# Last quarter of the second MLP matrix by Strassen's scheme, and the weight-block sums of all quarters on GpSimd

## What is computed

```
h = rms_norm(x, norm2_w[l])
x = x + jnp.square(jax.nn.relu(h @ w_up[l])) @ w_down[l]     # w_up 1024 x 4096, w_down 4096 x 1024
```

## Time and profile before

| | |
|---|---|
| median of three runs | 1588.47 us |
| profiled execution, span | 1587.5 us |
| TensorE busy | 1575.3 us, 99% |
| VectorE busy | 1011.7 us, 64% |
| ScalarE busy | 724.0 us, 46% |
| GpSimd busy | 0.2 us |
| share of TensorE in the chain that ended last | 95% |
| granted TensorE clock, mean | 0.999 |

### The profile page before, as it was taken

One profiled execution on the slowest core, in us unless ns is written; L12 is line 12 of the kernel. 1 busy time (PEld: TensorE's weight loads), 2 busy tenths in 40 slices (PEclk: granted clock), 3 DMA queues, 4 the chain that ended last, 5 costly groups with the idle time before them and its releaser, 6 DMA issues.

```text
span 1587.5 us, 21133 instructions
## 1 busy us (share of the span) xinstructions
PE 1575.3 (99%) x7576; PEld 1293.4 (81%) x7576; DVE 1011.7 (64%) x1431; ACT 724.0 (46%) x1109; POOL 0.2 (0%) x4
## 2 busy tenths in 40 slices
PE   8999999999999999999999999999999999999999
PEld 7877778888888888888887777788888888888887
DVE  5577774554456868696356776655455587787952
ACT  5557552323337363645345566432233464636350
POOL 0000000000000000000000000000000000000000
PEclk9999999999999999999999999999999999999999
DMA  6321222333351322323022212133323514141401
GB/s 225 112 81 54 84 76 80 106 107 102 108 188 54 124 89 106 107 86 131 9 72 98 89 54 81 53 107 106 106 80 106 186 54 163 50 159 54 156 4 53
DMA packets 109319, 153.22 MB, mean 97 GB/s; under 512 B 5120, under 2 KB 81440, under 8 KB 109216
## 3 DMA queue, kind: packets, MB, share of 16 engines
q1 hardware_dynamic: 108496, 151.27, 28.7%
q10 hardware_dynamic: 720, 0.61, 0.1%
HBM read 149.77 MB, written 2.10 MB: 96 GB/s over the span
## 4 chain that ended last, share of the span: by engine, by line
PE 95%; DVE 2%; ACT 1%; DMA 1%; issue 0%; SPq 0%; DVEq 0%; ACTq 0%
PE acc L541 19%; PE acc L543 19%; PE acc L542 19%; PE acc L563 6%; PE acc L565 6%; PE acc L564 6%; PE acc L592 5%; PE acc L594 5%; PE acc L593 5%; PE bank L729 1%; PE bank L748 1%; PE bank L740 1%; DMA raw<-in_w_in_dram 1%; PE bank L609 1%; DVE wl_rows L1051 1%; PE bank L701 0%
## 5 line engine op out<-in xcount | busy, mean ns | idle before, releaser
L541 PE MATMUL acc<-uh,wh 128*128 128x512 f32 x1152 | 452.8, 393 | 4.1 <-DVEq L1145 4.0
L543 PE MATMUL acc<-uh,wl 128*128 128x512 f32 x1152 | 449.1, 390 | 0.0
L542 PE MATMUL acc<-ul,wh 128*128 128x512 f32 x1152 | 449.1, 390 | 0.0
L541 PEld LDWEIGHTS acc<-uh,wh 128*128 128x128 f32 x1152 | 216.6, 188 | 53.7 <-issue 5.4
L827 ACT ACTIVATE wh<-raw 128x1024 fp32r<-128x1024 f32 x142 | 150.5, 1060 | 230.8 <-PE acc L543 151.3
L543 PEld LDWEIGHTS acc<-uh,wl 128*128 128x128 f32 x1152 | 216.6, 188 | 45.7
L542 PEld LDWEIGHTS acc<-ul,wh 128*128 128x128 f32 x1152 | 216.8, 188 | 44.1
L1051 DVE TENSOR_TENSOR wl<-raw,wh 128x1024 fp32r<-128x1024 f32 x142 | 174.0, 1225 | 82.4 <-ACT wh L827 71.4
L827 ACT ACTIVATE wh_rows<-raw_down 128x1024 fp32r<-128x1024 f32 x100 | 106.2, 1062 | 134.4 <-PE acc L594 35.2
L1051 DVE TENSOR_TENSOR wl_rows<-raw_down,wh_rows 128x1024 fp32r<-128x1024 f32 x100 | 122.5, 1225 | 59.3 <-ACT wh_rows L827 51.6
L1081 DVE TENSOR_TENSOR gate_tanh<-acc,rsqrt_rows 128x512 f32<-128x512 f32 x48 | 33.2, 691 | 116.2 <-PE acc L543 116.0
(11 more groups left out here) (235 smaller groups left out, 2449.1 us busy)
## 6 DMA issues: line engine op xcount, KB each, us to landing
raw<-in_w_in_dram SPq DMA_DIRECT2D x39, 1024.0 KB, 5.2
raw<-in_w_up_dram SPq DMA_DIRECT2D x32, 1024.0 KB, 5.7
raw_down<-in_w_down_dram SPq DMA_DIRECT2D x32, 1024.0 KB, 8.6
raw_branch<-in_w_in_dram SPq DMA_DIRECT2D x12, 1024.0 KB, 5.0
raw_branch<-in_w_branch_dram SPq DMA_DIRECT2D x12, 1024.0 KB, 5.0
raw_branch<-in_w_o_dram SPq DMA_DIRECT2D x8, 1024.0 KB, 5.0
x_tokens<-in_x_dram SPq DMA_DIRECT2D x8, 256.0 KB, 8.1
raw_kv<-in_w_in_dram SPq DMA_DIRECT2D x4, 512.0 KB, 4.8
```

What stands on the lines that cost most here:

```text
L541: nc.tensor.matmul(a[:], wh[slot][:, k, :], right_h, start=at_k == 0, stop=False)
L542: nc.tensor.matmul(a[:], wh[slot][:, k, :], right_l, start=False, stop=False)
L543: last = nc.tensor.matmul(a[:], wl[slot][:, k, :], right_h, start=False, stop=at_k == n - 1)
```

## The change

The last quarter becomes Strassen's scheme too: 14 `dn` units (`dn42` to `dn55`) take the place of `db` and `da`, with their hidden sums and with tiles that go into x directly where the running sums have already been folded. The words `ta` to `td` leave VectorE, and GpSimd makes the same eight sums in each of the eight quarters. The lists of all three engines are new from `wa3` on, and so is the order in which x is sent out.

```diff
-       + ([f"dn{14 * q + i}" for i in range(PRODUCTS * PAIRS)] if q < QUARTERS - 1 else
-          [f"{half}{i}" for half in ("db", "da") for i in range(4)])]
+       + [f"dn{14 * q + i}" for i in range(PRODUCTS * PAIRS)]]
...
-dn30 dn31 dn32 dn33 dn34 dn35 dn36 dn37 dn38 dn39 dn40 dn41 up24 up25 up26 up27 up28 up29 up30 up31 db0 db1 db2 db3
-da0.01 UT4 UT5 UT6 UT7 da0.23 da1 da2 da3""".split()
+dn30 dn31 dn32 dn33 dn34 dn35 dn36 dn37 dn38 dn39 dn40 dn41 up24 up25 up26 up27 up28 up29 up30 up31 dn42 dn43 dn44
+dn45 dn46 dn47 dn48 dn49 dn50 dn51 dn52 dn53 UT4 UT5 UT6 UT7 dn54 dn55""".split()
...
 ACT_LATE, third and fourth quarter:
++dn24 +dn25 +dn26 +dn27 +up16 +up17 rl16 hh16 +up18 rl17 +up19 +up20 +up21 +up22 rl18 rl19 dh2 hh17 hh18 hh19 +up23
+rl20 rl21 hh20 +dn28 +dn29 sh8 +dn30 sh9 rl22 +dn31 rl23 +dn32 sh10 hh21 +dn33 sh11 +dn34 +dn35 +dn36 +dn37 +dn38
++dn39 hh22 +dn40 hh23 +dn41 +up24 +up25 +up26 rl24 +up27 rl25 +up28 hh24 +up29 rl26 hh25 +up30 hh26 rl27 +up31 dh3
+rl28 +dn42 hh27 hh28 sh12 rl29 +dn43 hh29 sh13 rl30 hh30 +dn44 sh14 rl31 +dn45 hh31 sh15 +dn46 +dn47 +dn48 +dn49 +dn50
++dn51 +dn52 +dn53 +dn54 +dn55 UT4 +gq0 +gq1 UT5 UT6 UT7 +gk0""".split()
...
 DVE_LATE, third and fourth quarter:
++dn27 rs25 +up16 rs26 +up17 +up18 +up19 rs27 +up20 +up21 hl16 df2 +up22 dl2 hl17 +up23 hl18 su8 hl19 +dn28 su9 +dn29
+sl8 su10 hl20 sl9 +dn30 +dn31 +dn32 su11 rs28 sl10 rs29 sl11 +dn33 rs30 +dn34 hl21 rs31 +dn35 +dn36 rs32 +dn37 rs33
++dn38 rs35 +dn39 rs34 hl22 rs36 +dn40 hl23 rs37 +dn41 +up24 rs39 fo7 rs38 rs41 +up25 rs40 +up26 +up27 +up28 +up29 hl24
+fo6 hl25 +up30 hl26 df3 +up31 su12 hl27 +dn42 dl3 sl12 hl28 su13 hl29 sl13 +dn43 su14 +dn44 hl30 sl14 su15 +dn45 sl15
+rs42 +dn46 +dn47 hl31 rs43 +dn48 rs45 fo0 rs44 fo1 rs46 +dn49 rs47 +dn50 +dn51 rs48 +dn52 rs49 +dn53 fo3 fo4 fo2 +dn54
+rs50 rs51 rs52 +dn55 UT4 +gq0 +gq1 UT5 UT6 UT7 rs53 fo5 rs54 rs55 +gk0""".split()
...
-X_TILES = [(_t, _half) for _half in (1, 0) for _t in range(TT)]
+X_TILES = [(0, 1), (2, 1), (1, 1), (3, 1), (0, 0), (1, 0), (2, 0), (3, 0)]
...
+        @block.gpsimd
+        def _(pool):
+            G = nc.gpsimd
+            for l in range(DEPTH):
+                for q in range(QUARTERS):
+                    n = l * QUARTERS + q
...
+                    def split_by(place, pair):
+                        pool.wait_ge(lo_done, unit_at(l, f"dn{14 * q + 2 * place + pair}") + 1)
+
+                    for pair in range(PAIRS):
+                        b11, b12, b21, b22 = blocks(pair)
+                        pool.wait_ge(down_full[pair], (n + 1) * 32)
+                        G.tensor_tensor(b12, b22, b12, ALU.subtract).then_inc(b12_summed, 1)
+                    for pair in range(PAIRS):
+                        b11, b12, b21, b22 = blocks(pair)
+                        split_by(0, pair)
+                        pool.wait_ge(b12_summed, 2 * n + pair + 1)
+                        G.tensor_tensor(b11, b12, b11, ALU.add).then_inc(b11_summed, 1)
+                    for pair in range(PAIRS):
+                        b11, b12, b21, b22 = blocks(pair)
+                        split_by(2, pair)
+                        pool.wait_ge(b11_summed, 2 * n + pair + 1)
+                        G.tensor_tensor(b22, b22, b11, ALU.subtract).then_inc(b22_summed, 1)
+                    for pair in range(PAIRS):
+                        b11, b12, b21, b22 = blocks(pair)
+                        split_by(5, pair)
+                        G.tensor_tensor(b21, b21, b11, ALU.subtract).then_inc(b21_summed, 1)
...
                 def down_sums(q, place, t):
 
-                    i = PRODUCT[place]
+                    i, last = PRODUCT[place], q == QUARTERS - 1
                     a, free = tile_ready(dve, l, f"p{PRODUCTS * q + place}", t)
                     if i in (1, 5, 6):
                         row, half = {1: (0, 0), 5: (0, 1), 6: (1, 0)}[i]
                         scaled_into_x(row, t, half, a[:]).then_inc(free, 1)
+                        if last and i != 5:
+                            V.drain().then_inc(x_upd, 1)
+                        return
+                    if last and i == 3:
+                        scaled_into_x(0, t, 1, a[:])
+                        scaled_into_x(1, t, 1, a[:]).then_inc(free, 1)
+                        V.drain().then_inc(x_upd, 2)
                         return
...
-                    elif kind in ("ta", "tb", "tc", "td"):
-                        n, pair = l * QUARTERS + i // 2, i % 2
...
-                        if kind == "ta":
-                            dve.wait_ge(down_full[pair], (n + 1) * 32)
-                            V.tensor_tensor(b12, b22, b12, ALU.subtract).then_inc(b12_summed, 1)
```

More of the change, by code:

```diff
@@ L33 @@
 WARM = 12
-TOKEN_KINDS = ("kva", "sq", "gv", "gr", "wa", "wb", "db", "da")
+TOKEN_KINDS = ("kva", "sq", "gv", "gr", "wa", "wb")
 PRODUCTS = 7
@@ L93 @@
[L93 to L109, removed]
@@ L110 @@
-hl25 fo6 fo7 +up30 hl26 +up31 hl27 +db0 hl28 +db1 hl29 +db2 hl30 +db3 hl31 +da0 +da1 +da2 ry0 ry1 ry2 ry3 +da3 UT4 UT5
-UT6 UT7 +gq0 +gq1 +gk0 rz0 rz1 rz2 rz3""".split()
+dn30 dn31 dn32 dn33 dn34 dn35 dn36 dn37 dn38 dn39 dn40 dn41 up24 up25 up26 up27 up28 up29 up30 up31 dn42 dn43 dn44
+dn45 dn46 dn47 dn48 dn49 dn50 dn51 dn52 dn53 UT4 UT5 UT6 UT7 dn54 dn55""".split()
+ACT_LATE = """+wa3 +wb0 V0 +wb1 +wb2 +wb3 +up0 V1 V2 V3 +up1 sq0 +up2 sq1 sq2 V4 V5 V6 V7 +up3 sq3 rl0 +up4 rl1 hh0 hh1 rl2 hh2 +up5
@@ L816, in split_high @@
                         act.wait_ge({2: b11_summed, 3: b22_summed, 4: b12_summed, 6: b21_summed}[i],
-                                    2 * (l * (QUARTERS - 1) + q) + pair + 1)
-                elif u[0] == "d":
-                    act.wait_ge(down_full[step_of(u)[1] % 2], (l + 1) * QUARTERS * 32)
+                                    2 * (l * QUARTERS + q) + pair + 1)
                 else:
@@ L1488, in _ @@
                         k = i % BK
-                        dve.wait_ge(sums_hi, l * (QUARTERS - 1) * BK + i + 1)
+                        dve.wait_ge(sums_hi, l * QUARTERS * BK + i + 1)
                         V.tensor_tensor(hs[1][:, k], hs_sum[:, k], hs[0][:, k].bitcast(f32),
                                         ALU.subtract).then_inc(sums_ready, 1)
-                    elif kind in ("ta", "tb", "tc", "td"):
-                        n, pair = l * QUARTERS + i // 2, i % 2
-                        b11, b12 = down[pair][:, :, 0, 0:SEQ], down[pair][:, :, 0, SEQ:]
-                        b21, b22 = down[pair][:, :, 1, 0:SEQ], down[pair][:, :, 1, SEQ:]
-                        if kind == "ta":
-                            dve.wait_ge(down_full[pair], (n + 1) * 32)
-                            V.tensor_tensor(b12, b22, b12, ALU.subtract).then_inc(b12_summed, 1)
-                        elif kind == "tb":
-                            V.tensor_tensor(b11, b12, b11, ALU.add).then_inc(b11_summed, 1)
-                        elif kind == "tc":
-                            V.tensor_tensor(b21, b21, b11, ALU.subtract).then_inc(b21_summed, 1)
-                        else:
-                            V.tensor_tensor(b22, b22, b11, ALU.subtract).then_inc(b22_summed, 1)
                     elif kind == "fo":
@@ L1508, in _ @@
                         down_sums(i // 14, i % 14 // 2, i % 2)
-                    elif kind in ("ry", "rz"):
-                        half = int(kind == "ry")
-                        a, free = tile_ready(dve, l, ("da", "db")[half], i)
-                        scaled_into_x(i // 2, i % 2, half, a[:]).then_inc(free, 1)
-                        V.drain().then_inc(x_upd, 1)
 def constants():
```

39 lines of the change are left out of this document (19 added, 20 removed).

## The result

The changed kernel takes 1683.24 us (median of four runs, 1682.10 to 1685.03) against 1588.56 for the kernel before on the same chip: 1.0597 times as long, 95% interval 1.0582 to 1.0612. That is 94.7 us more where I forecast 22.5, and 41 us beyond the upper end of my range.

A forecast was written before the change was run, and what follows sets the result against it. TensorE's matmul count times pace was taken as the bound, with VectorE full in the MLP. 1587.5 - 10.9 (matmuls) + 16.2 (first three quarters) + 17.1 (last) = 1609.9; the median stands 1.0 above, so 1611, range 1578 to 1642.

The forecast's parts named there:

- The length of a sum: GpSimd weight sums of 128x1024 float32: bounded by 1.23 and 2.45 us, taken as 1.5 us each.
- Then VectorE catches up, and the b21 sums fall beside tiles: Third quarter's product, after the second b22 sum: no more stall than the 2.7 us reached by `dn35`.
- Free sums, and still a stall in the last product: 1.8 and 0.2 us: Last product, GpSimd at no cost: TensorE stalls 1.8 us at layer 0's transposes, 0.2 in layer 1 for `dn54`'s banks.
- Latency covered: GpSimd sums, even at 2.45 us, finish before TensorE needs them; those for `dn36` and `dn40` have some 8 us.
- Held up or side by side: VectorE beside GpSimd: each sum costs between nothing and its length; the forecast took the full hold-up, 1600 to 1643, chance 0.48.
- The third quarter by hand: Third quarter's product, worked step by step: stall of 2.7 us at sums of 1.5, 1.5 at 1.23, 6.4 at 2.45.
- laid out much like the third: Second quarter taken as like the third, first checked for the long sum (6.4 us): six stages at 2.7, 16.2 us.
- The last quarter: Last product stages, both layers together: stalls of 13.7, 21.3 and 26.9 us for sums of 1.23, 1.84 and 2.45; 17.1 at 1.5.
- The sum for short sums: Whole kernel with GpSimd sums of 1.23 us: 1588.5 - 10.9 + 9 + 13.7 = 1600 us.
- side by side: Rival: GpSimd's sums cost VectorE nothing, or GpSimd is the one that waits; 1579.6 us, chance 0.38.
- half a hold-up: Rival: GpSimd and VectorE share, each slowed in part, 0.5 to 1.2 us a sum; 1584 to 1600, chance 0.10.
- the one of sums over 5.3 us: Rival: GpSimd sums so long that TensorE waits for the splits of `dn40` and `dn41`; over 1600 us, chance 0.04.

The follow-up runs named there:

- the first experiment: The changed kernel with each of the 64 GpSimd sums cut from 512 columns of each row block to the first 8: 1586.73 us, ratio 0.9987.

## Why the prediction was wrong

The mechanism and the place were right, the size was not; for the direction I had hardly better than an even chance (0.54). Three steps failed. The length of a sum was put at 1.5 us and is 2.40. "Then VectorE catches up, and the b21 sums fall beside tiles" stopped the sum of a quarter halfway. And the `up` stages (10.3 us) and the slower matmuls behind a wait (some 17 us) had no term at all. Step by step:

- **48 matmuls, 10.9 us less.** Right. The pace under it is read from the earlier trace rows: 168 matmuls in 38.08 us, 0.2267 from one start to the next. There are 7528 matmuls now, and where nothing holds them the stages of the first experiment show 38.1 us, the old pace.
- **VectorE's own work, 12 us less.** Right to 2 us (1001.5 in place of 1011.7, with sums of hardly any length).
- **Free sums, and still a stall in the last product: 1.8 and 0.2 us.** Right in kind, somewhat too small. The last-quarter kernel with sums of no length shows 2.3 us in both layers, and 1583.95 us where 1579.6 was worked out. With the new orders it is 1586.7: the microseconds in the `up` stages, in the next layer's start and behind the last matmul, named with the first experiment, are places that I had not gone through.
- **Latency covered.** Right: no wait of TensorE names GpSimd. ScalarE waits 51 us in total for the b21 sums, but none of VectorE's waits follows from that.
- **Held up or side by side.** I took the hold-up, and that is what the chip does here: 2.67 us for a step of 0.43, while a tile with a PSUM input keeps its 0.69. No row before showed GpSimd beside VectorE, so both the hold-up and the tiles' freedom from it were assumptions of mine, and it took these runs to show them. They also show that a fill, which only writes, doesn't hold a step with both inputs in SBUF (0.43 us beside a fill of 0.95).
- **The length of a sum.** Wrong, and the first cause of the miss. I bounded it by 1.23 and 2.45 and took 1.5, near the VectorE row, since that was the only measured one. It is 2.40, so the upper end of the bound was the better estimate. (A copy with one input takes 1.05 us; that a sum reads its operands in turn, as my bound of twice 1.225 took it, no row and no run shows.) By my own steps the length is worth 32 us, 1643 for 2.45 against 1611.
- **The third quarter by hand.** Right for its first half, and wrong in the words "Then VectorE catches up, and the b21 sums fall beside tiles". With 2.45 in place of 1.5 in each hold, the steps of the prediction put the end of `dn30`'s low split at 7.2 (measured 7.5), of `rs28` at 14.6 (14.7) and of the low splits of `dn33` and `dn34` at 18.8 and 22.6 (18.9 and 22.4). That gives 6.4 us of stall, and `dn35` does start 6.5 us late. But VectorE doesn't catch up, and a b21 sum is longer than the tile that it starts beside. The split behind the tile, quoted above, is held to 2.69 us and `hl22` to 2.14. TensorE waits 1.33 us for the tile behind that split, and 2.22 for `hl23`, which VectorE reaches only after `hl22` and the split of `dn40`. With what the next point shows, 6.5 us become 12.4. Without the b21 sums this stage takes 46.0 us in place of 50.5.
- **The other two quarters "laid out much like the third".** Only roughly: 11.2 and 9.0 us beside 12.4 in layer 0, where my figure for the long sum was 6.4 in each.
- **The last quarter.** For 2.45 I had 14.2 us in layer 0 and 12.7 in layer 1; measured are 17.2 and 14.6. In layer 1 `dn54` starts 12.75 us late, just what I had for `rs50`, whose bank it needs; the rest comes behind it, at the slower pace of the next point. This hand calculation, carried through to its end, held.
- **The `up` stages.** I had no term for them. They took 10.3 us more than before, 1.1 of it also with sums of hardly any length.
- **The pace after a wait.** Left out of the prediction. I added waits to a pace of 0.227 us and took that pace as fixed. The timeline of TensorE behind one of the waits:

```profile
739.13 0.47 PE L588 MATMUL acc<-wh_rows,hidden_hi 128*128 128x512 f32 x1 [2.22 <-DVE hidden_lo L1497]
739.44 0.59 PE L589 MATMUL acc<-wh_rows,hidden_lo 128*128 128x512 f32 x1
739.82 0.63 PE L590 MATMUL acc<-wl_rows,hidden_hi 128*128 128x512 f32 x1
740.25 0.63 PE L588 MATMUL acc<-wh_rows,hidden_hi 128*128 128x512 f32 x1
740.67 0.63 PE L589 MATMUL acc<-wh_rows,hidden_lo 128*128 128x512 f32 x1
```

From 739.47 on the granted clock is 0.50 for 3.4 us, and the starts come to 0.43 us apart: each of these matmuls costs 0.2 us more, and `dn39` takes 4.42 us in place of 2.72. It doesn't happen behind every wait. In layer 1 the third quarter has the same two waits (1.37 and 2.21 us), and its clock stays at 1.00:

```profile
1533.54:1581.79 48.25, 40.52 (x169) 30.82 (x168) 42.82 (x41) 19.67 (x21) 12.73 (x6) 1.00 0.12 44
```

It takes 2.3 us less than its twin in layer 0, 1.6 of them in `dn39`. The granted clock of the four stages above is 0.93, 0.97, 0.91 and 0.94 where it was 1.00. Taken as (1 - clock) x length that is 3.4 + 1.5 + 5.1 + 3.2 = 13.2 of their 55.4 us of loss; in all eight product stages it comes to some 20. That is an upper estimate, because part of the low clock falls into the waits themselves. Added up from the trace, what the matmuls at a granted clock of 0.50 have over 0.227 us from start to start, those behind a wait left out, is 16.5 us of the 94.6.

- **The sum for short sums.** 1600 us at 1.23 was too low too: with sums of 1.29 us the kernel takes 1625. The third quarter's product stage in layer 0 lost 4.2 us where I had 1.5: 2.2 by `dn35`, and the rest in the half that I hadn't gone through, with the clock at 1.00. So even with the length right my method would have ended 25 to 40 us low: 1643 for 2.45, against 1683.

Put together, by the differences between kernels: the 48 matmuls -10.9; stalls that remain with sums of hardly any length +9.1; the length of the sums +96.5. The forecast had -10.9, +2.0 (part of its sum for the last quarter) and +31.3. Of the missing 65 us of the last term the length of a sum explains 32 (1643 against 1611). The other way round, by stages: over 1643 the changed kernel has 40 us. The six product stages of the first three quarters hold 24.4 of them (62.8 for 38.4), the two last ones 4.9 (31.8 for 26.9), and the `up` stages 10.3. The slower pace, some 17 us, is spread over these and is no term beside them; no run changes the clock alone.

Two rivals are refuted, side by side (1580) and half a hold-up (1584 to 1600), both by the steps of 2.67 us; the one of sums over 5.3 us, by their 2.40. None of the kernels with whole sums beats the kernel before. The nearest is the last quarter with VectorE's sums, 11 us slower. Sums in pieces in the old orders, and a more even order for the last quarter, were not tried.

## What to carry to other kernels

An idle GpSimd was no free capacity beside a full VectorE: VectorE's steps that read both inputs from SBUF were held by GpSimd's sums, which read from there too (2.67 us for a step of 0.43), so each sum was like a step put into VectorE's list at a time that nobody chose, twice as long as the same step on VectorE itself (2.40 us against 1.23). If it has to be done, three things helped here: VectorE steps with an operand in PSUM kept their length beside a sum (0.69 us), sums in short pieces took back 43 us, and in the old orders, with 12 us of lead, a product stage lost about a fifth of what it lost in the new ones. And when stalls are worked out, carry each stage to its end, also past the point where "it catches up", go through the stages beside it, and leave a term for the slower pace that can come with a wait: here 0.43 us from start to start in place of 0.227, at a granted clock of 0.50, beside ten waits of 1.8 to 5.9 us.

## What the runs showed of the hardware

- Length on GpSimd for float32 on 128 partitions, both inputs in SBUF, undisturbed: 2.40 us for 1024 elements a row, 1.29 for 512, 0.74 for 256, 0.22 for 16; a copy of 1024 1.05, a fill of 1024 0.96. The same sum on VectorE is 1.23.
- A GpSimd instruction that reads one operand holds VectorE's two-SBUF-input steps just as one that reads two (0.43 us became 1.29 beside a copy of 1.05, and 2.67 beside a sum of 2.40). A fill doesn't (0.43 beside a fill of 0.95). The one VectorE step with a single input from SBUF that met a fill (128x4, `squares_x_sums`) took 0.95 in place of 0.17; two copies out of PSUM that met one kept their 0.69.
- In these traces it works in both directions, and the one that comes second waits for the end of the first: sums of 16 elements take 0.22 us in the median, but five of the 16 b12 sums start beside a VectorE split, and their group has a mean of 0.41. The longest, 1.07 us, starts 0.22 us into a split and ends 0.08 us after it.
- A held instruction is recorded as busy (2.67 us for a step of 0.43). 110 us of VectorE's 1111.8 us were waiting, by the difference from the kernel with sums of hardly any length; in the profile of the changed kernel alone it shows in the distance of a group's mean from its usual length.
- In the changed kernel, between the first `up` stage and the end of layer 1's last product, the granted clock fell to half ten times, for 3.4 or 6.8 us each, beside waits of TensorE of 1.8 to 5.9 us; before, it fell in no stage of the MLP. A wait of 2.2 us went with a fall in layer 0 and with none in layer 1.
